# RWKV preparation: VectorE masks the first Gram block before it writes the finished tile's output, and the key products between the two first M transposes

## What is computed

```python
def step(S, inp):
    rt, wt, kt, vt, kkt, at = inp
    sa = jnp.einsum("bhvk,bhk->bhv", S, -kkt)
    S = S * wt[:, :, None, :] + sa[..., None] * (kkt * at)[:, :, None, :] + vt[..., None] * kt[:, :, None, :]
    return S, jnp.einsum("bhvk,bhk->bhv", S, rt)
```

## Time and profile before

| | |
|---|---|
| median of 3 runs | 3747.95 us (3745.85 to 3748.66) |
| the profiled execution | 3745.45 us, span 3743.6 us |
| mean granted TensorE clock | 0.940 |
| the RWKV stage with these loops | about 2918 to 3455 us of the span |
| one tile of it, third to eighth | about 65 us |

### The profile page before, as it was taken

How to read it: one execution, slowest core, us unless ns; L and a number is a source line. 1 busy time by engine, 2 the same in 40 slices (tenths; PEclk the granted TensorE clock), 3 DMA queues, 4 the chain that set the end, 5 groups by cost and what they waited for, 6 DMA issues and landing times. The chain is left out here.

```text
span 3743.6 us, 59561 instructions
## 1 busy us (share of the span) xinstructions
PE 3431.3 (92%) x25914; PEld 2501.4 (67%) x25914; DVE 918.3 (25%) x2050; ACT 637.9 (17%) x1431; POOL 225.2 (6%) x198
## 2 busy tenths in 40 slices
PE   6999996899999999999998799999989788788998
PEld 4777774688778877976456654444464577777887
DVE  0200016201000000001504513431031444543460
ACT  1010013201000100001313420000021334332100
POOL 0000000000000000000002210000000131221000
PEclk8999997899999999999998889999979898888999
DMA  9567841287778778776100113233310100003340
GB/s 380 222 254 309 309 153 43 82 296 258 260 266 289 261 258 297 255 264 228 56 34 2 64 61 124 112 135 123 129 70 37 38 22 13 22 3 126 124 157 23
DMA packets 86231, 576.46 MB, mean 154 GB/s; under 512 B 9488, under 2 KB 13584, under 8 KB 18192
## 3 DMA queue, kind: packets, MB, share of 16 engines
q1 hardware_dynamic: 82576, 568.27, 41.5%
q10 hardware_dynamic: 3456, 5.24, 0.4%
HBM read 567.19 MB, written 6.29 MB: 153 GB/s over the span
## 5 line engine op out<-in xcount | busy, mean ns | idle before, releaser
L258 PE MATMUL ps<-H,ring 128*128 128x256 f32 (+1 forms) x3600 | 1055.1, 455 | 16.8 <-ACT H L525 8.9
L258 PEld LDWEIGHTS ps<-H,ring 128*128 128x128 f32 x3600 | 692.7, 193 | 384.5 <-issue 317.2
L1271 PE MATMUL ps<-W,ring 128*128 128x128 f32 x5632 | 631.0, 275 | 10.0 <-ACT W L1297 10.0
L1271 PEld LDWEIGHTS ps<-W,ring 128*128 128x128 f32 x5632 | 629.5, 192 | 11.5 <-issue 11.5
L258 PE MATMUL ps<-W,ring 128*128 128x256 f32 (+1 forms) x1488 | 468.6, 476 | 10.4 <-DVE W L2392 8.0
L258 PEld LDWEIGHTS ps<-W,ring 128*128 128x128 f32 x1488 | 284.2, 192 | 198.2 <-issue 171.6
L1283 PE MATMUL ps<-ring,W 128*128 128x512 f32 x704 | 303.5, 592 | 0.0
L1283 PEld LDWEIGHTS ps<-ring,W 128*128 128x128 f32 x704 | 133.1, 190 | 164.5 <-issue 164.5
L1326 DVE TENSOR_TENSOR W<-ps,W 128x128 f32<-128x128 f32 x176 | 51.4, 292 | 620.5 <-PE ps L1271 620.5
L1528 DVE SCALAR_TENSOR_TENSOR W<-ps,vec,W 128x189 f32<-128x189 f32 (+3 forms) x396 | 173.3, 438 | 14.0
L2913 POOL TENSOR_TENSOR ring<-ring 128x512 f32<-128x512 f32 x96 | 124.4, 1312 | 558.8 <-DVE ring L2998 471.6
(11 more groups left out here) (387 smaller groups left out, 2777.5 us busy)
## 6 DMA issues: line engine op xcount, KB each, us to landing
ring<-weights SPq DMA_DIRECT2D x528, 1024.0 KB, 4.8
rkv<-W ACTq DMA_DIRECT2D x16, 256.0 KB, 2.0
ring<-rkv SPq DMA_DIRECT2D x8, 512.0 KB, 3.5
X<-tokens SPq DMA_DIRECT2D x1, 2048.0 KB, 8.5
ring<-rw_tiles SPq DMA_DIRECT2D x8, 256.0 KB, 5.2
const<-constants SPq DMA_DIRECT2D x1, 1168.0 KB, 10.8
rkv<-W ACTq DMA_DIRECT2D x8, 128.0 KB, 2.5
ring<-rkv SPq DMA_DIRECT2D x8, 128.0 KB, 3.6
```

What stands on the lines that cost most here:

```text
L258: mm = pe.matmul(out(o), lhsT=k.ring[:, k.slot(at), p * P:(p + 1) * P], rhs=rhs(kk), start=kk == 0, stop=kk == kt - 1)
L1271: mm = pe.matmul(k.ps[:, o % 4, 0:P], lhsT=self.weights(u)[:, i * P:(i + 1) * P], rhs=moe.Hg[:, kk, :], start=kk == 0, stop=kk == KD - 1)
```

## The change

Three things move in VectorE's block; no instruction is added or removed, and no other engine's block is touched. The masks of direction 0, now in a function `masked_grams`, move ahead of state 2, and state 2 ahead of the rest of the output and of Rt. The masks of direction 1 stay behind Rt. The key products' masks move from behind M of both directions to between them.

```diff
@@ -2931,6 +2931,12 @@
                     g = sc.G[s % 2][:, a:b + 1:b - a].unsqueeze(2).to_broadcast([P, 2, CH])
                     dve.tensor_tensor(sc.hat[(i + 1) % 2], ps[:, sc.U[0]:sc.U[1] + 1, 0:CH], g, ALU.mult).then_inc(sem["hat"], 1)
 
+            def masked_grams(j, z):
+                dve.wait_ge(sem["gram"], 2 * j + z + 1)
+                for h in range(2):
+                    dve.tensor_tensor(sc.LK[z][:, :, h], ps[:, ((0, 1), (2, 0))[z][h], :].rearrange("p (i b t) -> p i b t", i=2, t=CH),
+                                      sc.strict[z].unsqueeze(1).unsqueeze(1).to_broadcast([P, 2, 4, CH]), ALU.mult).then_inc(sem["lk"], 1)
+
             for j in range(TILES + 2):
                 s, q, prep = j - 1, j - 2, j < TILES
                 rkv = sc.rkv[j % 2]
@@ -2976,6 +2982,9 @@
                         dve.tensor_tensor(sc.bv[j % 3], ps[:, 2, S:2 * S], v_, ALU.mult).then_inc(sem["bv"], 1)
                         if q >= 0:
                             after(dve.scalar_tensor_tensor(sc.d, sc.d, sc.col(q, 6), ps[:, 2, 0:S], ALU.mult, ALU.mult))
+                if prep:
+                    masked_grams(j, 0)
+                next_state(s, 2)
                 if q >= 0:
                     if not prep:
                         dve.wait_ge(sem["rest"], j + 1)
@@ -2989,25 +2998,21 @@
                                                 r_.rearrange("p (c t) -> p c t", t=CH), sc.eR[z], ALU.mult)
                         ins.then_inc(sem["r"], 1) if z else ins.then_inc(sem["dve"], 1)
                     order[0] += 1
-                next_state(s, 2)
-                for z in range(2):
-                    if prep:
-                        dve.wait_ge(sem["gram"], 2 * j + z + 1)
-                        for h in range(2):
-                            out = sc.LK[z][:, :, h]
-                            dve.tensor_tensor(out, ps[:, ((0, 1), (2, 0))[z][h], :].rearrange("p (i b t) -> p i b t", i=2, t=CH),
-                                              sc.strict[z].unsqueeze(1).unsqueeze(1).to_broadcast([P, 2, 4, CH]), ALU.mult).then_inc(sem["lk"], 1)
+                if prep:
+                    masked_grams(j, 1)
                 next_state(s, 3)
                 if prep:
                     for z in range(2):
                         dve.wait_ge(sem["ot"], 12 * j + z + 1)
                         after(dve.tensor_tensor(sc.MT[j % 2][z], sc.OT[z][0], sc.unit.unsqueeze(1).to_broadcast([P, 8, CH]), ALU.add))
                         dve.transpose(flat(sc.M[z]), flat(sc.MT[j % 2][z])).then_inc(sem["m0"], 1)
-                    dve.wait_ge(sem["gram_r"], j + 1)
-                    for h in range(2):
-                        out = sc.BKR[j % 2][:, h].rearrange("p z i (b t) -> p z (i b) t", b=2)
-                        dve.tensor_tensor(out, ps[:, 1 + h, :].rearrange("p (z n t) -> p z n t", z=2, t=CH),
-                                          sc.upto.unsqueeze(2).to_broadcast([P, 2, 4, CH]), ALU.mult).then_inc(sem["bkr"], 1)
+                        if z:
+                            break
+                        dve.wait_ge(sem["gram_r"], j + 1)
+                        for h in range(2):
+                            out = sc.BKR[j % 2][:, h].rearrange("p z i (b t) -> p z (i b) t", b=2)
+                            dve.tensor_tensor(out, ps[:, 1 + h, :].rearrange("p (z n t) -> p z n t", z=2, t=CH),
+                                              sc.upto.unsqueeze(2).to_broadcast([P, 2, 4, CH]), ALU.mult).then_inc(sem["bkr"], 1)
                 next_state(s, 4)
                 for l in range(1, 6):
                     if prep:
```

## The result

| | before | after |
|---|---|---|
| median (runs of this comparison) | 3746.90 us (4 runs, 3740.35 to 3748.66) | 3716.68 us (4 runs, 3716.53 to 3719.39) |
| the profiled execution, its span | 3745.45, 3743.6 us | 3716.74, 3714.9 us |
| mean granted TensorE clock | 0.940 | 0.945 |
| first mask of tile 2, of tile 7 | 3058.39, 3383.05 | 3048.17, 3355.72 |
| so one tile | 64.9 us | 61.5 us |

The ratio is 0.9925, with the 95% interval 0.991 to 0.9941: faster by 30 us. The forecast was 3726, its range 3716 to 3737.

The account below looks back on a forecast made before the run. TensorE's waits for VectorE's first mask and key products, 37 us over eight tiles, were taken as all the change could touch. Six tiles at 3.1, tile 1 1.4, tile 0 2, turns 0.2: 22.2 us, giving 3726, range 3716 to 3737.

Parts of the forecast that it names:

- A: Tile stretch from the start of BK of direction 1 to VectorE's key products; forecast gain 3.1 us a full tile.
- GpSimd beside the four moved operations: Between the masks on VectorE: GpSimd's level-0 mask holds up L2983 by 1.12 us; second mask 0.55 us earlier, not 1.67.
- The first rival: The four operations moved behind the first mask are not held up by GpSimd; 3718 to 3725 us; chance 17%.
- M of direction 0 meets the second operation: VectorE's first L3004 meets GpSimd's second operation, not its third, and ends at 3130.4 instead of 3132.19: 1.8 us won.
- This rival: L3004 still meets GpSimd's third operation, so 1.24 us a tile are not won; 3733 us; chance 10%.
- The key products between the M pairs: L3009 follows the first L3005, at 3131.07 instead of 3134.18; TensorE's eight transposes start 3.1 us earlier a tile.
- Neither rival: Clock stays half longer before key products: 3736 us, 10%; further half-clock stretches in level loop or next tile's start: 3765, 3%.
- The price that the rival put on half clock: Half clock held through key products, state step and four transposes: eight transposes 1.7 us late; 3736 us; chance 10%.
- The first wait: TensorE's wait before L2735 for VectorE's first mask: under 1 us a tile instead of 2.46.
- The mis-sized term: Everything outside A: no gain in the sum, only 0.83 us either way in most tiles for half-clock stretches.
- B: Rest of a tile, from VectorE's key products to the next tile's BK of direction 1; no gain in the sum.

Follow-up runs that it names:

- e3: The changed kernel with GpSimd's level-0 mask of direction 0 waiting for the fourth mask instead of the second; 3711.99 us, ratio 0.9911.
- e2: The kernel before with only the key products moved between the M pairs, masks and output as before; 3722.49 us, ratio 0.994.
- e10: The changed kernel with TensorE multiplying constants that nobody reads ahead of three waits in each tile; 3722.15 us, ratio 0.9938.
- e9: The kernel before with three more set-up memsets on VectorE ahead of the loop, nothing else changed; 3744.56 us, ratio 0.9996.
- e4: The changed kernel with three more set-up memsets on VectorE ahead of the loop, nothing else changed; 3717.49 us, ratio 0.9926.
- e7: The changed kernel with GpSimd's level-1 masks waiting for M of their direction; 3715.49 us, ratio 0.9916.

## Why the prediction was right, and where it wasn't

The mechanism was the one forecast, and its sum for A came out. That the total stayed in the range is in part luck: the rest of the tile gave 6 us that the sum didn't have, the time fell below the forecast's own range, and 1 us more would have put it outside the whole. The sum for A: 22.0 us for the eight tiles against 22.7 measured (2.22 and 1.44 in tiles 0 and 1 for 2 and 1.4; 3.10 to 3.20 in the other six for 3.1).

- **GpSimd beside the four moved operations.** Forecast by the row of L3004, between the bounds 0 and 1.12: L2983 some 1.6 us and the second mask 4.04 after the first. Measured 1.52 and 3.96. e3 shows the cause by taking it away. The first rival falls.
- **M of direction 0 meets the second operation.** Forecast: L3004 3.4 us after the second mask, ended 4.42 after it. Measured 3.37 and 4.41. The threshold came from one row ("later than 3.66 us" for state 3, so 3.86 for M 0.20 behind it); e2 puts it for M between 3.72 and 3.86. This rival was real, though not here.
- **The key products between the M pairs.** They follow 1.71 us after M's start, and TensorE is waiting no longer in tile 3; over the eight tiles its wait is 4.4 us instead of 16.3. The hold on the second L3007 (1.05 us) costs nothing that can be seen, as taken.
- **The clock.** Neither rival came: the level loop stayed at 1.00, and the half clock in A fell from 56.9 us in eight tiles to 30.3. e10 shows the other direction alone: a full clock in all of A wins nothing there. The price that the rival put on half clock, 1.7 us a tile, is what e9 shows for A of the kernel before, though by another path (the second Gram product and the late meeting). What a longer half-clock stretch would cost in the changed kernel stays open, as no kernel forced it; so does what the Trainium skill, "TensorE: Matmul & The Clock Gate", "Part 4: PE-mode transpose", says of transposes, as no kernel changed them alone.
- **The first wait.** "Under 1 us" was wrong, it is 1.72 in tile 3. In the changed kernel the first Gram product ran at full clock (1.16 us instead of 1.75), so TensorE was done early and waited for VectorE, which is the bound there. The length of the wait didn't measure the cost.
- **The wait that I didn't name.** With the second mask 4 us behind the first, four transposes are done before it, and TensorE stands 1.77 us. I had used this ("only eight are left behind it") and not called it a wait; state 3 came as forecast.
- **The mis-sized term.** Everything outside A stood in the sum as zero, with a margin of 0.83 us a tile either way. It gave 6.0 us, 5.5 of them in B: nearly the whole of the 6.6 us between 3723.3 and the profiled 3716.74. The tiles' time at half clock explains them in size: over tiles 1 to 6 B spent 44.0 us at half before and 33.9 after, by 0.33 a us 3.3 of the 4.4 us won there. That is a correlation, supported by e4, where the same program at another time shows the same law. The prediction had taken "the change takes waits away" only as a reason against a loss; the thirteen traces show it as a gain, 2.9 us or more in B with the key products' move. In tile 1 of before the half-clock stretch at the level loop's start, which stays away in the changed kernel, accounts for 1.5 (10.39 us to the first transpose instead of 8.90). How much of the other 2.6 us is the change, and how much the phase that it happened to meet, isn't shown. In e7 (against the changed kernel) and e9 (against before) the same term had the other sign.

The other 2.5 us of the distance are those by which the median of before (3747.95) stood above its profiled execution. The changed kernel shows no such distance, and the kernel before measured 3744.36, 3745.15, 3746.31 and 3746.90 in its comparisons.

## What to carry to other kernels

When an operation with two SBUF inputs is moved on VectorE, look first at what GpSimd does at its new place, and price it at the rest of that GpSimd operation; better still, hand GpSimd its work only when VectorE has passed its critical operations, if GpSimd's readers are late enough (here that was worth 14 us more). Cost the path by the engine that ends each stretch: waits of TensorE that grew or appeared here cost nothing, as VectorE set the pace. And in a pipeline near TensorE's limit give the forecast a term for the unchanged part of the loop too, which moved by up to 3 us a tile, most of it with where the half-clock stretches fell.

## What the hardware showed that I had not expected

- A difference of 0.14 us in arrival (3.72 or 3.86 us after the mask) turned an addition of 0.69 us into one of 1.79. GpSimd runs its operations back to back, and VectorE got in only between two of them: in before, after, e2 and e3, each of the 55 additions of M begun inside a GpSimd operation ended 0.55 us (at most 0.60) after that operation did.
- The full clock bought nothing where another engine ended the stretch: with TensorE kept busy at clock 1.00 A stayed at 10.20 us. And in B, where TensorE is busy over 80% of the time, an us at half clock went with 0.33 us of time and not with half of it.
- Where the clock decided which GpSimd operation was met, it cost more than its own slowness: in the kernel before, half clock in the second Gram product costs 0.83 us, and the later meeting that can follow another 1.24, of which 0.36 come back at the second M.
